# Gate and up products of six feed-forward networks by 2x2 blocks: seven products in place of eight

## The reference, cut to what matters

```
def _swiglu(x, wi, wo):
    a, b = jnp.split(x @ wi, 2, axis=-1)
    return (jax.nn.silu(a) * b) @ wo
...
for layer in range(DEPTH):
    h = h + 0.5 * _swiglu(_rms_norm(h, ln_ffn1[layer]), ffn1_wi[layer], ffn1_wo[layer])
    ... attention ...
    h = h + 0.5 * _swiglu(_rms_norm(h, ln_ffn2[layer]), ffn2_wi[layer], ffn2_wo[layer])
```

## Time and profile before

| | us |
|---|---|
| median of the runs | 3736.02 |
| the profiled execution, device time | 3736.37 |
| its span in the profile | 3734.7 |
| PE busy | 3566.8 |
| DVE busy | 1741.1 |
| ACT busy | 1300.1 |
| POOL busy | 440.0 |

### The profile page before, as it was taken

How to read it: one execution, slowest core, us unless ns; L and a number is a source line. 1 busy time by engine, 2 the same in 40 slices (tenths; PEclk the granted TensorE clock), 3 DMA queues, 4 the chain that set the end, 5 groups by cost and what they waited for, 6 DMA issues and landing times. The chain is left out here.

```text
span 3734.7 us, 50566 instructions
## 1 busy us (share of the span) xinstructions
PE 3566.8 (96%) x20104; PEld 2920.9 (78%) x20104; DVE 1741.1 (47%) x2492; ACT 1300.1 (35%) x1793; POOL 440.0 (12%) x465
## 2 busy tenths in 40 slices
PE   8999799799999999989999999999999899799998
PEld 7999777699999999755547888888744477678886
DVE  5442466544434443266625443443377533545433
ACT  4332266433323332134525432342110243324421
POOL 0000222100000000010006400000144233220000
PEclk9999899899999999989999999999999999999999
DMA  4322311022222222300013222222212421233222
GB/s 168 135 88 85 122 55 51 18 91 90 83 85 102 90 86 78 136 26 23 1 34 113 101 88 103 101 90 90 101 51 85 120 78 51 107 108 108 94 85 84
DMA packets 116172, 318.07 MB, mean 85 GB/s; under 512 B 13815, under 2 KB 56951, under 8 KB 100052
## 3 DMA queue, kind: packets, MB, share of 16 engines
q1 hardware_dynamic: 116052, 316.51, 25.0%
HBM read 307.98 MB, written 17.01 MB: 87 GB/s over the span
## 5 line engine op out<-in xcount | busy, mean ns | idle before, releaser
L332 PE MATMUL acc<-fb_xh,fb_wh 128*128 128x264 f32 x1408 | 287.8, 286 | 5.5 <-DVE fb_wl L489 5.5
L332 PE MATMUL acc<-fb_xl,fb_wh 128*128 128x264 f32 x1408 | 288.1, 286 | 0.0
L332 PE MATMUL acc<-fb_xh,fb_wl 128*128 128x264 f32 x1408 | 287.7, 286 | 0.0
L332 PE MATMUL acc<-fd_xh,fd_wh 128*128 128x512 f32 x704 | 275.6, 391 | 5.5 <-DVE fd_wl L489 5.5
L332 PE MATMUL acc<-fd_xl,fd_wh 128*128 128x512 f32 x704 | 274.6, 390 | 0.0
L332 PE MATMUL acc<-fd_xh,fd_wl 128*128 128x512 f32 x704 | 274.6, 390 | 0.0
L332 PEld LDWEIGHTS acc<-fb_xh,fb_wh 128*128 128x128 f32 x1408 | 220.1, 189 | 5.8 <-DVE fb_wl L489 5.7
L407 ACT ACTIVATE fb_wh<-fb_raw 128x2048 fp32r<-128x2048 f32 (+1 forms) x74 | 124.7, 1686 | 286.9 <-PE acc L391 173.8
L332 PEld LDWEIGHTS acc<-fb_xl,fb_wh 128*128 128x128 f32 x1408 | 219.3, 189 | 0.0
L332 PEld LDWEIGHTS acc<-fb_xh,fb_wl 128*128 128x128 f32 x1408 | 219.0, 189 | 0.0
L484 DVE TENSOR_TENSOR fb_wl<-fb_raw,fb_wh 128x2048 fp32r<-128x2048 f32 (+1 forms) x74 | 148.3, 2004 | 141.5 <-ACT fb_wh L407 140.6
(11 more groups left out here) (532 smaller groups left out, 8766.0 us busy)
## 6 DMA issues: line engine op xcount, KB each, us to landing
fb_raw<-wi_dram SPq DMA_DIRECT2D x42, 1024.0 KB, 4.8
fd_raw<-wi_dram SPq DMA_DIRECT2D x42, 1024.0 KB, 4.8
fb_raw<-wo_dram SPq DMA_DIRECT2D x32, 704.0 KB, 4.0
fd_raw<-wo_dram SPq DMA_DIRECT2D x32, 704.0 KB, 4.0
...
```

Source lines behind the costliest of these rows:

```text
L332: last = pe.matmul(acc[:, up_base(p, b) + 2 * a + q, 0:w], x[:, k, a, :], part[:, k, t0:t0 + w], start=k == 0 and part is xh and x is wv, ...
```

## The change

The gate and up products of chunks 2 to 21 of each network are made by blocks. The tokens are cut into two halves of columns (264 or 256), the 1024 channels of D into two halves, and gate and up are the two halves of the output: a 2x2 by 2x2 product. Seven products of blocks take the place of eight. Each is 4 (channels) x 3 matmuls, 12 in all, so a chunk has 84 matmuls of 264 or 256 columns. For this, sums of blocks are made: four of the weights of each chunk, on GpSimd (`weight_sums`: S1, S2, S4, and one in place in `raw`), and four of the tokens once per network (`sums_of_x`). The names of the products are numbers: 1, 6, 5, 2, 3, 7, 4 in the order of work. Products 2, 1, 4 and 7 use blocks that lie in `raw` (7 the one summed in place), 5, 6 and 3 use `sum_`.

The weights now pass through a ring of 8 buffers of 128x512 (`RING`): ScalarE rounds the block of the product 8 places on as soon as TensorE is done with a product. The rest is made on VectorE for products 6, 5, 2, 3 and 7 and on GpSimd for 1, 4 and all of the down product (`by_pool`). The results of the seven products are put together on VectorE (`seven_out`), one PSUM bank each, in turn over 8 banks. The first two chunks of a network stay plain products, now in pieces of half the tokens also for 512 tokens.

The down product is made in four parts (`DOWN`: chunks 0 to 5, 6 to 10, 11 to 16, 17 to 21), each behind the up chunks that it needs and two more, and added to `h` four times; `gh` and `gl` hold 8 chunks. `raw` has three buffers. The loops are written out. The rotation tables are made by GpSimd in `dsa_stage`, in a part of `mix`, stored to DRAM, and loaded again in `scan_stage`.

```diff
-HF = FC // 2
-UP, DN = KC * 2 * P, HF * P
...
+w, HK, RING, LEAD, RAW, SLOTS_ = n // 2, KC // 2, 8, 2, 3, 8
...
+DOWN = ((0, 6), (6, HF), (HF, HF + 6), (HF + 6, FC))
+jobs = []
+for d, (u0, u1) in enumerate(DOWN):
+    made_up = sum(kind == "up" for kind, _, _ in jobs)
+    jobs += [("up", u, 0) for u in range(made_up, min(u1 + 2, FC))]
+    jobs += [("dn", d, c) for c in range(KC)]
+JOBS, TAIL = len(jobs), len(jobs) - KC
+A11, A21, A12, A22, D0_, D1_ = 11, 21, 12, 22, 100, 101
+PLAIN, SEVEN = (A11, A21, A12, A22), (1, 6, 5, 2, 3, 7, 4)
+order = [(i, p) for i in range(2) for p in PLAIN]
+for i in range(2, JOBS):
+    order += [(i, p) for p in (SEVEN if jobs[i][0] == "up" else (D0_, D1_))]
+PER = len(order)
+place = {ip: x for x, ip in enumerate(order)}
+W_PART = {A11: (0, 0), A21: (1, 0), A12: (0, 1), A22: (1, 1), 1: (0, 0), 2: (0, 1), 4: (1, 1), 7: (1, 0)}
+W_SUM = {5: 0, 6: 1, 3: 2}
+X_PART = {1: 0, 5: 1, 2: 2, 3: 3, 6: 4, 7: 5, 4: 6}
+def by_pool(i, p):
+    return i == 0 or (i > 1 and p in (1, 4, D0_, D1_))
...
         @block.gpsimd
         def _(pool):
-            arm(pool, *following)
-            if ahead:
-                ahead.work(pool)
+            def weight_sums(net, i, p):
+                a11, a21 = block_of(net, i, 0, 0), block_of(net, i, 1, 0)
+                a12, a22 = block_of(net, i, 0, 1), block_of(net, i, 1, 1)
+                s1, s2, s4 = (weights_of(net, i, q) for q in (5, 6, 3))
+                if p == 6:
+                    raw_landed(pool, net, i, 1)
+                    last_read(net, i, 5)
+                    pool.tensor_tensor(s1, a21, a22, ALU.add).then_inc(sums, 1)
+                    last_read(net, i, 6)
+                    pool.drain()
+                    pool.tensor_tensor(s2, s1, a11, ALU.subtract).then_inc(sums, 1)
+                elif p == 3:
+                    last_read(net, i, 3)
+                    pool.drain()
+                    pool.tensor_tensor(s4, a12, s2, ALU.subtract).then_inc(sums, 1)
+                elif p == 7:
+                    pool.tensor_tensor(a21, a11, a21, ALU.subtract).then_inc(sums, 1)
+            def sums_of_x(net, k):
+                f = pairs[k % 2]
+                pool.wait_ge(eo, 1 + HK * net + k + 1)
+                pool.tensor_tensor(f[:, 1, :], f[:, 7, :], f[:, 0, :], ALU.subtract)
+                pool.tensor_tensor(f[:, 5, :], f[:, 3, :], f[:, 7, :], ALU.subtract)
+                pool.drain()
+                pool.tensor_tensor(f[:, 4, :], f[:, 3, :], f[:, 1, :], ALU.subtract)
+                pool.drain()
+                pool.tensor_tensor(f[:, 6, :], f[:, 2, :], f[:, 4, :], ALU.subtract).then_inc(t_on, 1)
+            for p in PLAIN:
+                rest_of_weights(0, 0, p)
+            for net in range(NETS):
+                for k in range(HK):
+                    sums_of_x(net, k)
+                pool.wait_ge(t_lo, 1 + HK * (net + 1))
+                for i, p in order[RING:RING + LEAD]:
+                    weight_sums(net, i, p)
+                for x in range(PER):
+                    if x + RING + LEAD < PER:
+                        weight_sums(net, *order[x + RING + LEAD])
+                    e = PER * net + x + RING
+                    if e < PER * NETS and by_pool(*order[e % PER]):
+                        rest_of_weights(e // PER, *order[e % PER])
+            arm(pool, *following)
...
+            def second_chunk(net):
...
+                pe.wait_ge(rooted, 1 + net + 1)
+                for k in range(KC):
+                    last = plain_step(net, 1, 1, k)
+                last.then_inc(made, 4)
+            def product(net, i, p):
+                bank_wait(pe, net, i, p)
+                lo_wait(pe, net, i, p)
+                if i == 2 and p == 6:
+                    pe.wait_ge(t_lo, 1 + HK * (net + 1))
+                for m in range(HK):
+                    ms = slice(m * P, (m + 1) * P)
+                    for x, part in ((wh, xh), (wh, xl), (wl, xh)):
+                        last = pe.matmul(acc[:, bank(net, i, p), 0:w], entry(x, net, i, p)[:, ms],
+                                         part[:, X_PART[p], m, :], start=m == 0 and x is wh and part is xh,
+                                         stop=m == HK - 1 and x is wl)
...
+            def round_weights(net, i, p):
+                e = PER * net + place[i, p]
+                if e >= RING:
+                    act.wait_ge(made, made_by((e - RING) // PER, *order[(e - RING) % PER]))
+                if p in W_SUM or (p == 7):
+                    act.wait_ge(sums, sum_count(net, i, p))
+                else:
+                    raw_landed(act, net, i, W_PART[p][1] if p in W_PART else 0)
+                act.activation(by_chunk(entry(wh, net, i, p)), weights_of(net, i, p), ACT.Copy).then_inc(hi, 1)
...
+            for net in range(NETS):
+                if net:
+                    lo_wait(act, net - 1, TAIL - 1, 7)
+                    for k in range(2):
+                        scaled_pair(net, k)
+                for k in range(HK):
+                    round_sums_of_x(net, k)
+                    if k + 2 < HK:
+                        scaled_pair(net, k + 2)
+                for x, (i, p) in enumerate(order):
+                    kind, u, c = jobs[i]
+                    if p == 1:
+                        copy_first(net, i)
+                    if i > 1 and p in (1, D0_) and jobs[i - 1][0] == "up":
+                        round_hidden(net, jobs[i - 1][1])
+                    e = PER * net + x + RING
+                    if e < PER * NETS:
+                        round_weights(e // PER, *order[e % PER])
+                    if x == 3:
+                        act.wait_ge(summed, 1 + net + 1)
+                        act.activation(folded(rstd[:, :], n), acc[:, bank(net, 1, A12):
+                                                                  bank(net, 1, A12) + np_, 0:wide], ACT.Sqrt,
+                                       scale=1.0 / D, bias=eps_t[:, :]).then_inc(rooted, 1)
+                        silu(net, 0)
+                        round_hidden(net, 0)
+                    elif x == 7:
+                        silu(net, 1)
+                    elif p == 7:
+                        silu(net, i)
...
-            def split_weights(b, n_, done):
-                dve.wait_ge(rounded, done)
-                dve.tensor_tensor(wl[:, b, 0:n_], raw[:, b, 0:n_], wh[:, b, 0:n_].bitcast(F32),
-                                  ALU.subtract).then_inc(split, 1)
+            def rest_of_weights(net, i, p):
+                dve.wait_ge(hi, 1 + PER * net + place[i, p] + 1)
+                dve.tensor_tensor(by_chunk(entry(wl, net, i, p)), weights_of(net, i, p),
+                                  by_chunk(entry(wh, net, i, p).bitcast(F32)), ALU.subtract).then_inc(lo_d, 1)
...
+            def seven_out(net, i, p):
+                of = acc[:, bank(net, i, p), 0:w]
+                dve.wait_ge(made, made_by(net, i, p))
+                if p == 6:
+                    dve.wait_ge(copied, 1 + of_act * net + jobs[i][1] - 1)
+                    dve.tensor_tensor(u2, of, x1, ALU.add).then_inc(outs, 1)
+                    dve.drain()
+                elif p == 5:
+                    dve.tensor_tensor(u4, of, u2, ALU.add).then_inc(outs, 1)
+                    dve.drain()
+                elif p == 2:
+                    dve.tensor_tensor(gate[:, 0:w], of, x1, ALU.add).then_inc(outs, 1)
+                    dve.drain()
+                elif p == 3:
+                    dve.tensor_tensor(gate[:, w:n], of, u4, ALU.add).then_inc(outs, 1)
+                    dve.drain()
+                    dve.tensor_tensor(gate[:, :], gate[:, :], rstd[:, :], ALU.mult).then_inc(gated, 1)
+                elif p == 7:
+                    dve.tensor_tensor(u3, of, u2, ALU.add)
+                    dve.tensor_tensor(up[:, w:n], of, u4, ALU.add).then_inc(outs, 1)
+                    dve.drain()
+                elif p == 4:
+                    dve.tensor_tensor(up[:, 0:w], of, u3, ALU.add).then_inc(outs, 1)
+                    dve.drain()
+                    dve.tensor_tensor(up[:, :], up[:, :], rstd[:, :], ALU.mult)
+                    dve.drain()
+                    hidden(net, jobs[i][1])
...
+                for x, (i, p) in enumerate(order):
+                    kind, u, c = jobs[i]
+                    if i > 1 and p in (6, D0_) and jobs[i - 1][0] == "up":
+                        rest_of_hidden(net, jobs[i - 1][1])
+                    if x == 3 or x == 7:
+                        plain_out(net, i)
+                    elif p in (6, 5, 2, 3, 7, 4) and kind == "up" and i > 1:
+                        seven_out(net, i, p)
+                    elif p == D1_:
+                        down_out(net, i)
+                    e = PER * net + x + RING
+                    if e < PER * NETS and not by_pool(*order[e % PER]):
+                        rest_of_weights(e // PER, *order[e % PER])
...
-        arm(pool, "fd_", "t_")
+        arm(pool, "fd_")
```

(6 more changed lines are left out.)

908 lines of the change are left out of this document (494 added, 414 removed).

## The result

The changed kernel takes 3951.39 us (median of 4 runs, 3949.18 to 3953.13), the kernel before beside it 3736.4: a ratio of 1.0575, interval 1.0557 to 1.0593. The forecast was 3955.

What follows compares the result with a forecast made beforehand. TensorE, busy 96% of the span, was taken as the bound, with VectorE later in up phases. Networks 193, starts 10, clock 10 and tables 6 made +219 on 3736.37: 3955 us, range 3760 to 4100.

Steps and rivals of the forecast that it cites:

- TensorE's saving: Up chunks with 84 matmuls: 29.4 us saved per network at 528 tokens, 14.3 at 512, 131 us in all.
- VectorE's lap: VectorE's time per chunk by blocks: 10.9 us of work and wait plus 3.3 beside GpSimd, 14.2; each chunk 4.0 late.
- hits: VectorE passes with two SBUF operands held up by GpSimd passes that read SBUF: 3.3 us per chunk.
- share of time: GpSimd busy 7.6 of some 14 us, so about half of nine VectorE passes meet it, 0.68 us each.
- Stretches: Runs of 6, 5, 6 and 3 up chunks by blocks: TensorE waits 18, 6, 10 and 0, 34 us per network.
- Root: Network start: TensorE's second chunk waits 14 us in a stage's first network, plus 3.5 for squares, 10 in its second.
- Last rest: Before a down part TensorE waits for the last hidden rest: 5 us per network.
- the clock: TensorE starts at 1.2 GHz after idling, 1.6 us lost each at six root waits: 10 us, bounds 0 and 20.
- Starts and tables: Four stages start 2.5 us later each, 10; rotation tables delay head stores in the attention stage, 6 us.
- interlock: Rival: GpSimd's passes fall into VectorE's waits, lap 12.2, 1.9 late; 3775 us, chance 0.14.
- faster: Rival: PE's products pace all three engines, lap 10.9, its 0.6 lateness covered by stock; 3690 us, chance 0.10.
- every pass meets: Rival: slower gapped reads keep GpSimd never free, lap 16.9, 6.6 late; 4205 us, chance 0.09.

Runs made afterwards that it cites:

- k1_small_pool: The changed kernel with GpSimd's six passes per gate and up chunk by blocks covering only 4 of each 128 columns; 3726.26 us.
- k6_small_sums: The changed kernel with only the four sums of weights per chunk covering 4 of each 128 columns, GpSimd's two rests whole; 3755.20 us.
- k13_writes: The changed kernel with each of GpSimd's four sums of weights replaced by four memsets of 128x128 over the same places; 3760.58 us.
- k4_dve_rests: The changed kernel with all seven rests of a chunk on VectorE, GpSimd keeping the sums of weights and down rests; 3987.75 us.
- k9_best: The changed kernel with the edits of k2_turn and k3_root, and 1/rms applied to the down product's parts instead of the up half; 3823.16 us, ratio 1.0234.
- k2_turn: The changed kernel with ScalarE's rounding of the hidden product moved behind the next product 6's weights, VectorE's rest behind product 6's pass; 3923.43 us.
- k3_root: The changed kernel with root and reciprocal taken behind the second of four steps of the sums of tokens; 3932.15 us.

## Why the prediction was right

**TensorE's saving.** Right: matmuls of 256 columns take 0.120 also in 84 rows on end (k1_small_pool). Those of 264 take 30.54 us for 252, so 0.1212, where I had 0.1224: 2 us more saved per network at 528 tokens. The figures of the Trainium skill, "TensorE: Matmul & The Clock Gate", section "Wait — 56ns, not 53.3ns?", by which it would be 109.2 and 112.5 ns, stay below both.

**VectorE's lap, 14.2 us (14.1 at 512).** Measured 14.07 in three laps. Own work 9.2, waits 1.22 + 0.16, hits 3.5, against 9.35, 1.4 and 3.3. k1_small_pool shows the first two together (10.59), k6_small_sums, k13_writes and k4_dve_rests show that the third goes with GpSimd's reads. But the way to 3.3 was partly luck. I took a share of time, half of nine passes at 0.68. What happens is a fixed pattern: each pass of GpSimd that reads SBUF meets one of VectorE, which loses 0.54 to 1.12 by where in GpSimd's pass it starts, unless VectorE is idle then. Two passes gave 1.3 and 1.7, four 3.4, six 3.5 with the pause and 4.1 to 4.4 without. The rule by share would have given k9_best 3.6 (eight passes x 0.68 x 7.6/11.5). For k2_turn I didn't even use it but left the hits at 3.4, and overrated it by 1.1 us per lap.

**Stretches, 34 us per network.** fb_, first network: 14.2 + 5.5 + 9.1 + 0 = 28.8, as lengths between PE's lines less 84 x 0.1212 per chunk; fd_, first: 14.9 + 5.6 + 11.3 + 0 = 31.8. I had 18 + 6 + 10 + 0. The first is too high: six laps 4.0 late are 24, of which 14 to 15 reach TensorE, so the ring's stock ahead of it is nearer 10 us than 6. In fa_ the second stretch lost 10.3 instead of 5.5; that stage also carries copies for the attention (`beside`) on the same queue as the weights. That this is the cause was not tried.

**Root, 14 + 3.5 and 10.** From the matmul that sums the squares, behind the first chunk, to the first product (before: to the third chunk) fb_ loses 18.1 and 13.5 us against before, fd_ 19.3 and 13.5, clock included: with my 1.6 for the clock it was 19 and 11.6. k3_root shows that it is not the root alone: without it 6 to 7 us remain for the banks.

**Last rest, 5, and the clock, 10 in all.** The wait is 4.2 to 4.5 us, but the last down part is 6.2 to 7.3 longer than the second, which has as many matmuls. The step that was mis-sized is the clock, for which I had counted the root waits only. The windows behind the wait of 4.55 us in ff_, and behind one of 2.35 us in that stage's second chunk, which I hadn't counted either:

```profile
3907.20:3910.00 2.80, 2.77 (x7) 2.19 (x8) 0.69 (x1) 0.78 (x2) 1.43 (x2) 0.50 0.10 38
3910.00:3915.00 5.00, 5.00 (x19) 4.02 (x18) 0.69 (x1) 1.56 (x4) 1.74 (x3) 0.79 0.22 66
...
3545.42:3550.30 4.88, 4.88 (x28) 4.88 (x29) 2.44 (x4) 2.37 (x4) 2.14 (x3) 0.65 0.62 215
```

PEclk 0.50, 1.2 GHz, for 4.9 us of the first two in all, and for 3.4 us of the third. By the granted clock in the trace TensorE works 86.5 us at 1.2 GHz in the four stages, where it worked 13.9 before: 28.0 behind the six root waits, 29.5 behind the six waits for the last rest, 13.6 in the second chunks of the four first networks, and the remaining 15.4 at the stages' starts, about as before. Half of it is lost, so 36 us more than before, where I had 10; behind a root wait it is 2.3 us and not my 1.6, for which I had used a window that ended at 1971.5, while the clock rose at 1972.4. The waits of 1.57 us within a lap left it at 1.00.

So the sum is near by errors that cancel. Over the six networks the stretches cost 188 us (I had 204), from the sum of squares to the first product 103, clock included (100), the last down part 41, clock included (30), and TensorE saves 137 (131). That makes 195 of the measured 204; of the other 9 some 5 lie in the first chunks, the rest I can't place.

**Starts and tables, 10 and 6.** The first matmul of fa_ comes 2.7 us later, and the waits for the first weights of the others are 3.1, 3.0 and 3.2 longer. Of these the attention ahead of fd_ shows all (3.2 more), what lies ahead of ff_ only 0.8; ahead of fb_ it is 5.4, of which 1.0 is a longer wait on `a_pd` and the rest was not traced. The tables cost nothing: on GpSimd they ran from 1811.5 to 1924.9, 113 us and not 138, while the store of head 10 came at 1946.7. I had taken the duration from fd_, where 15 of GpSimd's passes had grown to between 1.07 and 2.54 us beside VectorE's passes, its rests of 2.3 us above all, 31 us in all; in the attention stage none is over 1 us.

The rivals: interlock (3775) and faster (3690) fall with the hits in every lap; "every pass meets" was nearer to the mechanism than my own account, but its price counted nine hits where GpSimd has six passes.
